# Reading high and low input in one 512-column matmul in eight products of a network of five layers

## The reference

```python
for i in range(DEPTH):                       # DEPTH = 4
    h = rmsnorm(x, norm_mix_g[i])
    ...                                      # y = mixer(h) @ w_out
    x = x + y
    x = x + swiglu(rmsnorm(x, norm_ffn_g[i]), f_w13[i], f_w2[i])
```

## Time and profile before

| | us |
|---|---|
| median of 3 runs (lowest to highest) | 1989.76 (1988.86 to 1992.17) |
| span of the profiled execution | 1991.3 |
| four `out` products, first to last matmul | 22.8, 22.8, 24.3, 23.1 |
| four `down` products of the first block | 62.4 each |

### The profile page before, as it was taken

How to read it: one execution, slowest core, us unless ns; L and a number is a source line. 1 busy time by engine, 2 the same in 40 slices (tenths; PEclk the granted TensorE clock), 3 DMA queues, 4 the chain that set the end, 5 groups by cost and what they waited for, 6 DMA issues and landing times.

```text
span 1991.3 us, 38243 instructions
## 1 busy us (share of the span) xinstructions
PE 1875.5 (94%) x13712; PEld 1712.3 (86%) x13712; DVE 1317.5 (66%) x2067; ACT 969.0 (49%) x1265; POOL 231.9 (12%) x177
## 2 busy tenths in 40 slices
PE   7999997989999999988999999999989988999997
PEld 7999997857999995558999999999975964789997
DVE  6876666687766686657666688676661754386653
ACT  4457633644774353114773345763354634347641
POOL 0020033103001200003002103003102000030012
PEclk9999998979999999999999999999996999799998
DMA  6555654412556452104556455565540430245561
GB/s 200 169 169 189 208 172 176 136 38 85 180 189 199 155 193 73 48 0 131 187 192 197 154 173 179 183 206 174 183 136 0 179 106 1 85 151 179 175 201 63
DMA packets 77810, 289.56 MB, mean 145 GB/s; under 512 B 9611, under 2 KB 11948, under 8 KB 77356
## 3 DMA queue, kind: packets, MB, share of 16 engines
q1 hardware_dynamic: 77740, 288.64, 44.4%
HBM read 287.56 MB, written 1.05 MB: 145 GB/s over the span
## 4 chain that ended last, share of the span: by engine, by line
PE 74%; DVE 12%; POOL 5%; issue 3%; ACT 2%; DMA 1%; DVEq 1%; POOLq 1%; SPq 0%; ACTq 0%
PE bank L412 20%; PE bank L414 20%; PE bank L413 20%; DVE wlo L1276 4%; POOL sumsq L1257 3%; PE bank L574 2%; POOL square L1256 2%; PE bank L618 1%; PE bank L632 1%; PE bank L661 1%; PE bank L684 1%; DMA raw<-in_w 1%; PE bank L511 1%; PE bank L762 1%; DVE conv_cv L1380 1%
## 5 line engine op out<-in xcount | busy, mean ns | idle before, releaser
L412 PE MATMUL bank<-xh,whi 128*128 128x256 f32 (+1 forms) x2896 | 830.0, 287 | 22.8 <-DVE wlo L1276 19.9
L853 ACT CAST whi<-raw 128x1024 fp32r<-128x1024 f32 (+1 forms) x490 | 539.7, 1102 | 617.2 <-PE bank L414 564.1
L414 PE MATMUL bank<-xh,wlo 128*128 128x256 f32 (+1 forms) x2896 | 823.6, 284 | 0.0
L413 PE MATMUL bank<-xl,whi 128*128 128x256 f32 (+1 forms) x2896 | 823.1, 284 | 0.0
L1276 DVE TENSOR_TENSOR wlo<-raw,whi 128x1024 fp32r<-128x1024 f32 (+1 forms) x491 | 686.4, 1403 | 12.5 <-ACT whi L853 12.4
L412 PEld LDWEIGHTS bank<-xh,whi 128*128 128x128 f32 x2896 | 550.3, 190 | 29.9 <-issue 13.2
L414 PEld LDWEIGHTS bank<-xh,wlo 128*128 128x128 f32 x2896 | 551.0, 190 | 0.0
L413 PEld LDWEIGHTS bank<-xl,whi 128*128 128x128 f32 x2896 | 548.4, 189 | 1.3 <-issue 0.5
L414 PE MATMUL bank<-ffn_hh,wlo 128*128 128x256 f32 (+1 forms) x880 | 249.3, 283 | 0.0
L413 PE MATMUL bank<-ffn_hl,whi 128*128 128x256 f32 (+1 forms) x880 | 248.3, 282 | 0.0
L412 PE MATMUL bank<-ffn_hh,whi 128*128 128x256 f32 (+1 forms) x880 | 248.2, 282 | 0.0
(11 more groups left out here) (270 smaller groups left out, 2092.9 us busy)
## 6 DMA issues: line engine op xcount, KB each, us to landing
raw<-in_w SPq DMA_DIRECT2D x414, 512.0 KB, 3.5
raw<-in_w SPq DMA_DIRECT2D x80, 704.0 KB, 4.3
att_bias<-in_bias SPq DMA_DIRECT2D x1, 3072.0 KB, 11.3
hy_decay<-in_decay SPq DMA_DIRECT2D x4, 512.0 KB, 5.3
ret_tab<-in_ret_tab SPq DMA_DIRECT2D x1, 1216.0 KB, 5.9
mla_uq<-in_uq SPq DMA_DIRECT2D x1, 1152.0 KB, 7.1
x<-in_xT SPq DMA_DIRECT2D x1, 1024.0 KB, 5.8
hy_w<-in_filt_w SPq DMA_DIRECT2D x4, 256.0 KB, 4.3
```

The lines of the kernel that those rows point to most:

```text
L412: pe.matmul(ps, whi[:, slot, wc], hi[:, k, cols], start=first, stop=False)
L413: pe.matmul(ps, whi[:, slot, wc], lo[:, k, cols], start=False, stop=False)
L414: mm = pe.matmul(ps, wlo[:, slot, wc], hi[:, k, cols], start=False, stop=last)
L853: nc.scalar.copy(whi[:, p % RING, 0:k * P], raw[:, p % RING, 0:k * P]).then_inc(panel_hi, 1)
```

## The change

In the products `out0` to `out3` and `down0` to `down3` (`WIDE`), the high and the low part of an input lie side by side in one tensor, and one matmul of 2 x 256 columns reads both against `whi`: whi x high lands in columns 0 to 255 of the bank, whi x low in columns 256 to 511. wlo x high is a matmul of 256 columns as before. The two halves are put together by DVE, which adds the upper half of the bank to `x` and, after a `link`, the lower half. The other products still do three matmuls; only the places of their operands are other ones.

```diff
+WIDE = tuple(f"{kind}{layer}" for kind in ("out", "down") for layer in range(DEPTH))
...
-    xh = sb("xh", [P, C, L], F32R)
-    xl = sb("xl", [P, C, L], F32R)
+    xx = sb("xx", [P, C, 2, L], F32R)
...
                 ps = bank[(ph.b0 + tile) % 4][:, 0:cols.stop - cols.start]
+                both = bank[(ph.b0 + tile) % 4][:].rearrange("p (a b) -> p a b", a=2)
...
-                    pe.matmul(ps, whi[:, slot, wc], hi[:, k, cols], start=first, stop=False)
-                    pe.matmul(ps, whi[:, slot, wc], lo[:, k, cols], start=False, stop=False)
-                    mm = pe.matmul(ps, wlo[:, slot, wc], hi[:, k, cols], start=False, stop=last)
+                    hi, lo = pair[:, k, 0, cols], pair[:, k, 1, cols]
+                    if ph.wide:
+                        pe.matmul(both, whi[:, slot, wc], pair[:, k, :, cols], start=first, stop=False)
+                    else:
+                        pe.matmul(ps, whi[:, slot, wc], hi, start=first, stop=False)
+                        pe.matmul(ps, whi[:, slot, wc], lo, start=False, stop=False)
+                    mm = pe.matmul(ps, wlo[:, slot, wc], hi, start=False, stop=last)
...
-                    V.tensor_tensor(x[:, m, cols], x[:, m, cols], bank[(ph.b0 + tile) % 4][:, w],
-                                    ALU.add).then_inc(bank_free, 1)
+                    ps = bank[(ph.b0 + tile) % 4]
+                    if ph.wide:
+                        link(V.tensor_tensor(x[:, m, cols], x[:, m, cols], ps[:, SEQ:2 * SEQ], ALU.add))
+                    V.tensor_tensor(x[:, m, cols], x[:, m, cols], ps[:, w], ALU.add).then_inc(bank_free, 1)
...
-            dve_steps(ph, 0, ph.n, step)
+            dve_steps(ph, 0, ph.n, step, *((link, 2 if ph.k == K11 else 4) if ph.wide else ()))
```

More of the change, by code:

```diff
@@ L92, in __init__ @@
         self.tiles, self.block0 = tiles, block0
+        self.wide = name in WIDE
 def plan():
@@ L386, in _, with panel @@
     def _(pe):
-        def panel(ph, i, j, hi, lo, cols, ready):
+        def panel(ph, i, j, pair, cols, ready):
             slot = (ph.p0 + j) % RING
@@ L428, in total, with product @@
             mm.then_inc(norm_total, 1)
-        def product(name, hi, lo, cols, ready, norm=None):
+        def product(name, pair, cols, ready, norm=None):
             ph = PH[name]
@@ L434, in product @@
                 for j in range(4):
-                    panel(ph, 0, j, hi, lo, cols, ready)
+                    panel(ph, 0, j, pair, cols, ready)
                     if j == 0 and norm:
@@ L441, in product @@
                     for j in range(4):
-                        panel(ph, i, j, hi, lo, cols, ready)
+                        panel(ph, i, j, pair, cols, ready)
             else:
@@ L445, in product @@
                     for j in range(4):
-                        panel(ph, i, j, hi, lo, cols, ready)
+                        panel(ph, i, j, pair, cols, ready)
             for j in range(ph.n % 4):
-                panel(ph, rounds, j, hi, lo, cols, None)
+                panel(ph, rounds, j, pair, cols, None)
         def filter_layer(layer):
@@ L473, in attention_in @@
             for j in range(4):
-                panel(ph, 0, j, xh, xl, A, (x_lo, C * norm))
+                panel(ph, 0, j, xx, A, (x_lo, C * norm))
                 if j == 0:
@@ L480, in attention_in @@
                 for j in range(4):
-                    panel(ph, i, j, xh, xl, A, None)
+                    panel(ph, i, j, xx, A, None)
                     head_sums(i, (j + 2) % 4, 4 * i + j - 2)
             for j in range(4):
-                panel(ph, 4, j, xh, xl, A, None)
+                panel(ph, 4, j, xx, A, None)
                 if j < 2:
@@ L487, in attention_in @@
             for j in range(4):
-                panel(ph, 5, j, xh, xl, A, None)
+                panel(ph, 5, j, xx, A, None)
         def attention():
@@ L694, in gate_panels @@
                 for j in js:
-                    panel(PH["in_gate"], i, j, xh, xl, B, None)
+                    panel(PH["in_gate"], i, j, xx, B, None)
             def squares_sum(g, cn):
@@ L789, in _ @@
             else:
-                product(f"in{layer}", xh, xl, A, (x_lo, C * norm), norm)
+                product(f"in{layer}", xx, A, (x_lo, C * norm), norm)
             if layer == 0:
@@ L794, in _ @@
             bufs = {"conv": cm, "attention": at, "hyena": hy}[kind]
-            product(f"out{layer}", bufs["yh"], bufs["yl"], A, (y_lo, YBASE[f"in{layer}"]))
-            product(f"up{layer}", xh, xl, A, (x_lo, C * norm), norm)
+            product(f"out{layer}", bufs["yy"], A, (y_lo, YBASE[f"in{layer}"]))
+            product(f"up{layer}", xx, A, (x_lo, C * norm), norm)
             norm += 1
-            product(f"down{layer}", ffn["hh"], ffn["hl"], A, (hid_lo, FC * layer))
-        product("in_ret", xh, xl, B, (x_lo, C * norm), norm)
+            product(f"down{layer}", ffn["hh"], A, (hid_lo, FC * layer))
+        product("in_ret", xx, B, (x_lo, C * norm), norm)
         norm += 1
         retention()
-        product("in_mla", xh, xl, B, None)
+        product("in_mla", xx, B, None)
         latent()
[L804 to L807, removed]
+        product("ret_out", rt["yy"], B, None)
+        product("mla_out", ml["yy"], B, None)
+        product("w_o", mg["yy2"], B, (y_lo, YBASE["mrg"]))
+        product("up4", xx, B, (x_lo, C * norm), norm)
         norm += 1
-        product("down4", ffn["hh"], ffn["hl"], B, (hid_lo, FC * DEPTH))
+        product("down4", ffn["hh"], B, (hid_lo, FC * DEPTH))
         pe.wait_ge(sumsq_done, norm)
@@ L1175, in _ @@
                 first_taps(ph, 8, 8)
[L1176 removed]
+                y_high(ph, 16, 8, cm["yy"], A, YR[f"in{layer}"])
                 if layer == 0:
@@ L1290, in x_parts @@
         def x_parts(m, gain, cols, norm):
-            V.tensor_scalar(xh[:, m, cols], x[:, m, cols], gain, None, ALU.mult).then_inc(x_hi, 1)
+            V.tensor_scalar(xx[:, m, 0, cols], x[:, m, cols], gain, None, ALU.mult).then_inc(x_hi, 1)
             dve.wait_ge(x_hi, C * norm + m + 1)
-            V.scalar_tensor_tensor(out=xl[:, m, cols], in0=x[:, m, cols], scalar=gain,
-                                   in1=xh[:, m, cols].bitcast(F32), op0=ALU.mult,
+            V.scalar_tensor_tensor(out=xx[:, m, 1, cols], in0=x[:, m, cols], scalar=gain,
+                                   in1=xx[:, m, 0, cols].bitcast(F32), op0=ALU.mult,
                                    op1=ALU.subtract).then_inc(x_lo, 1)
```

26 lines of the change are left out of this document (13 added, 13 removed).

## The result

The changed kernel took 2010.9 us (median of 4 runs, 2006.8 to 2017.7), the one before 1989.4; the ratio is 1.0104, 95% interval 1.0083 to 1.0125. That is 21 us slower, where 14 were forecast with a range of 5 to 23. The profiled execution has a span of 2008.3 us.

What follows compares the result with a forecast made beforehand. The prediction took PE to bound `down` and DVE to bound `out`. Its terms, -7.6 - 0.35 + 17.6 + 1.8 + 2.5 = +13.95 us, put the median of 1989.8 at 2003.7 us, range 1995 to 2013.

Steps and rivals of the forecast that it cites:

- The bound, and the sign: PE bounds down and DVE bounds out, so the change was forecast slower, by 13.95 us in sum.
- The step of 3.56 us: In out, the second add lengthens DVE's step from 3.01 by 0.55 to 3.56 us, +17.6 us in all.
- POOL's wait for the high part: In out, POOL would wait 1.06 instead of 0.51 us a step for DVE's high part.
- Addresses: Panel matmuls that keep their shapes read other addresses, 0.5 ns each: +-4.7 us, put in the range only.
- The gain of 10.8 ns a chunk: On PE, a chunk takes 344.4 instead of 355.2 ns: -7.6 us over the 704 chunks of down.
- The rival by which the surplus goes with the columns: Wide matmul on PE takes 234.4 ns, gain only 2.4 ns a chunk, total 2009.9 us; chance 0.22.
- hardly grows with columns: On PE, the surplus, 11.7 ns at 256 columns and 12.3 at 272, is paid once a matmul; 12.7 for a wide one.
- The clock: Longer PE waits bring the lower clock level behind all four out, and a little longer: +2.5 us, between 0 and 6.
- The last adds of `down`: In each down only the eighth second add is not hidden behind PE: 4 x 0.46 = +1.8 us.
- 17.6 - 0.35 + 2.5: In and behind out: +17.6 us for DVE's adds, -0.35 for faster first panels on PE, +2.5 for the lower clock.

Runs made afterwards that it cites:

- x apart: The changed kernel, but xh and xl, the inputs of the other products, stay two tensors as before; ratio 1.0062 to the kernel before.
- layout, add only: The changed kernel with three matmuls a chunk instead of wide ones, and an unused scratch add with a wait in each step of out; ratio 1.0109 to the kernel before.
- layout alone: The changed kernel with high and low parts in one tensor, but no wide matmul and no second add; ratio 1.0071 to the kernel before.
- wide in `down` only: The changed kernel with wide matmuls and second add in the four down products alone, paired tensors everywhere; ratio 1.0081 to the kernel before.

## Why the prediction was right, point by point

**The bound, and the sign.** Right, and for the reason given: `out` is bound by DVE, and an add in each of its steps costs its full length while PE's saving there turns into waiting. An add in the kernel before is enough for the loss, and taking DVE off the path undoes it.

**The step of 3.56 us.** Measured 3.52 and 3.59; right in sum, not in its parts. The second add costs 0.45 (x apart: 3.46), not 0.55; the rest, 0.06 to 0.13, is the layout, which I had left out of `x_parts`. DVE computes other addresses there (the rows of the order show an ISA row in place of a REGISTER_ALU ahead of the low part); that these take the time was not tried by itself. POOL's wait for the high part, forecast at 1.06 us a step, is 1.00 to 1.02 in four steps of `out1` that follow each other.

**Addresses.** "Read other addresses ... +-4.7 us ... into the range, not the sum": this is the term that was sized by the wrong engine. On PE it was 0.6 ns a matmul, 2.1 us, in `up`, and as many ns the other way in `up4` (125.55 instead of 126.21). (The matmuls it goes over are 9,696 and not 9,312, which makes the 4.7 a 4.8.) On DVE it was a later high and low part, one step lost to POOL in `out1` and `out2` (0.6 us each), the same in six steps of `w_o`, which I hadn't looked at, and PE's longer wait behind it.

**The gain of 10.8 ns a chunk.** Too large: 355.2 - 350.0 = 5.2 ns, so 704 x 5.2 = -3.7 us at best instead of -7.6, and -3.0 in this profile. Not all of it comes from merging: with the new places and three matmuls a chunk ("layout, add only") each `down` takes 62.07 us from first to last start instead of 62.40, 353.3 ns a chunk, so merging saves 3.3 ns and the places 1.9. A wide matmul took 233.5 ns and its partner 116.5. The rival by which the surplus goes with the columns had 234.4, and it was the right one of the two for the price, though its partner was 2 ns faster than it said. 272 columns against 256 could not tell the two apart, and "hardly grows with columns" was misread from them: 11.7 and 12.3 ns grow by 0.6 over 16 columns, which carried on to 512 gives 21.3 and not the 12.7 of the sum.

**The clock.** +2.5 us was too small. From the start of DVE's last add in `out` to the fourth panel of `up` it was 11.8, 11.8, 10.9 and 10.9 us before, and 12.0, 12.8, 12.3 and 12.5 after: +4.3 us, of which my sum had the 2.5. A part of the 4.3 is chance: it is 49.5 us in all with the layout alone and 46.4 with wide in `down` only, whose instructions there are the same. Where the clock stayed up and POOL started earlier it was 10.1 in all four.

**The last adds of `down`**, +1.8 us: right. From the last matmul of `down` to the fourth panel of the product behind it, the four layers take 46.0 us together in each of the five kernels without the wide `down`, and 47.8 to 48.0 in all that have it.

Together: 17.6 - 0.35 + 2.5 was forecast between `out` and `up`, 22.3 came; -7.6 was forecast in `down`, -3.0 came; nothing was forecast for the rest of `up`, 2.1 came, nor for `w_o` and `up4`, 3.1 came. All these errors go the same way, 12.4 us together: they make +14 into +26, the 25.9 us between the profiles without retention, where the range ended at +23. That 2003.7 was low by 7 us only, and the time within the range, is in part luck: the four runs before, 1989 to 1992, all lie at or just under the slower of its two groups.

## What to carry to other kernels

Before work is moved from one engine to another, find for each stage which engine's step sets the pace: the same edit gained 3 us where TensorE was the bound, of which the last adds took 1.8 back, and lost 17 to 22 where VectorE was, though TensorE was busy 94% of the span. If only some readers need a new layout, leave the others as they are; here a layout that removed no work cost 0.7% by itself. Look at what a late chain does to the clock behind it: a wait of TensorE is paid once as a wait and again as slow matmuls.

## What was not expected of the hardware

- A shift of 0.01 to 0.08 us in the start of the low part decides who waits, VectorE or GpSimd: the same low part takes mostly 0.85 to 0.98 us, or 0.48 us.
- An fp32r matmul of 512 columns at 2.4 GHz takes 231.8 to 233.5 ns from start to start, one of 256 columns 116.5 to 121 by its neighbours and addresses, one of 272 about 125: the surplus over columns / 2.4 is 18 to 20, 10 to 14 and 12 ns.
- The same 169 matmuls of retention take 68.8 us at a mean clock of 0.73 or 61.9 at 0.81, and the executions of one program fall into two groups some 11 us apart. What sends an execution one way or the other is open.
